# Stick-breaking attention: suffix sums as pairs of float32r matmuls, the mask added on TensorE, and the weights kept in softplus form

## The reference

```
z = jnp.einsum('bqhd,bkhd->bhqk', qb, kk).astype(jnp.float32) * scale
...
mask = (k_pos[None, :] < q_pos[:, None])[None, None]
log_beta = jax.nn.log_sigmoid(z)
log_one_minus = jnp.where(mask, jax.nn.log_sigmoid(-z), 0.0)
suffix = lax.cumsum(log_one_minus, axis=3, reverse=True) - log_one_minus
A = jnp.where(mask, jnp.exp(log_beta + suffix), 0.0)
outs.append(jnp.einsum('bhqk,bkhd->bqhd', A.astype(v.dtype), vv))
```

## Time and profile before

| What | us |
|---|---|
| median of 3 runs | 4930.05 (4927.13 to 4930.28) |
| the profiled execution, its own time | 4933.49 |
| its span in the profile | 4931.4 |
| PE busy in the span | 4438.4 (90%) |
| DVE busy in the span | 2837.3 (58%) |
| ACT busy in the span | 1843.0 (37%) |

### The profile page before, as it was taken

One profiled execution on the slowest core, in us unless ns is written; L12 is line 12 of the kernel. 1 busy time (PEld: TensorE's weight loads), 2 busy tenths in 40 slices (PEclk: granted clock), 3 DMA queues, 4 the chain that ended last, 5 costly groups with the idle time before them and its releaser, 6 DMA issues. The chain is left out here.

```text
span 4931.4 us, 59891 instructions
## 1 busy us (share of the span) xinstructions
PE 4438.4 (90%) x22171; PEld 3698.0 (75%) x22171; DVE 2837.3 (58%) x5051; ACT 1843.0 (37%) x2602; POOL 413.9 (8%) x308
## 2 busy tenths in 40 slices
PE   7988888878998466999999996999999999899998
PEld 5867775645874256999999995766878877677887
DVE  0777776683436897888888885334343333444332
ACT  1655644443321033333333333346232233643322
POOL 0000000000002601232222320000000000000000
PEclk9999999999999798999999998999999999999999
DMA  7111111102221036777777771211323322122232
GB/s 261 56 39 39 35 35 43 39 13 90 90 77 61 10 137 229 280 269 281 271 277 280 270 278 63 72 48 45 101 90 98 95 75 66 37 73 92 95 96 84
DMA packets 195952, 578.14 MB, mean 117 GB/s; under 512 B 17328, under 2 KB 66736, under 8 KB 194352
## 3 DMA queue, kind: packets, MB, share of 16 engines
q1 hardware_dynamic: 157888, 433.77, 25.9%
q0 software_dynamic: 36864, 134.23, 8.0%
q10 hardware_dynamic: 1008, 7.55, 0.4%
HBM read 548.22 MB, written 27.26 MB: 117 GB/s over the span
## 5 line engine op out<-in xcount | busy, mean ns | idle before, releaser
L402 DVE TENSOR_TENSOR tile_rest<-tile_raw,tile_up 128x1024 fp32r<-128x1024 f32 (+2 forms) x288 | 338.6, 1180 | 781.9 <-ACT tile_up L393 781.6
L410 PE MATMUL layer_psum<-hn_up,tile_up 128*128 128x512 f32 x1344 | 535.0, 398 | 21.2 <-DVE hn_rest L497 21.2
L411 PE MATMUL layer_psum<-hn_up,tile_rest 128*128 128x512 f32 x1344 | 527.3, 392 | 0.0
L412 PE MATMUL layer_psum<-hn_rest,tile_up 128*128 128x512 f32 x1344 | 527.0, 392 | 0.0
L393 ACT ACTIVATE tile_up<-tile_raw 128x1024 fp32r<-128x1024 f32 (+2 forms) x288 | 291.4, 1018 | 369.1 <-PE layer_psum L412 368.5
L2186 PE MATMUL ex_psum<-ex_t_up,ex_u_up 128*128 128x384 f32 x1024 | 344.5, 336 | 10.5 <-ACT ex_prod L2260 6.2
L2204 PE MATMUL ex_psum<-ex_prod_up,ex_v_up 128*128 128x384 f32 x1024 | 342.9, 335 | 3.9 <-DVE xT L2326 3.9
L2187 PE MATMUL ex_psum<-ex_t_up,ex_u_rest 128*128 128x384 f32 x1024 | 344.0, 336 | 0.0
L2188 PE MATMUL ex_psum<-ex_t_rest,ex_u_up 128*128 128x384 f32 x1024 | 343.9, 336 | 0.0
L2206 PE MATMUL ex_psum<-ex_prod_rest,ex_v_up 128*128 128x384 f32 x1024 | 342.6, 335 | 0.0
L2205 PE MATMUL ex_psum<-ex_prod_up,ex_v_rest 128*128 128x384 f32 x1024 | 342.6, 335 | 0.0
(11 more groups left out here) (440 smaller groups left out, 10140.1 us busy)
## 6 DMA issues: line engine op xcount, KB each, us to landing
ex_u<-in_peer_u SPq DMA_DIRECT2D x128, 512.0 KB, 6.8
tT<-in_peer_v SPq DMA_DIRECT2D x128, 512.0 KB, 7.4
tile_raw<-in_w_gu SPq DMA_DIRECT2D x88, 512.0 KB, 3.5
xT<-in_w_head SPq DMA_DIRECT2D x56, 512.0 KB, 3.5
mod_w<-in_w_ada SPq DMA_DIRECT2D x48, 512.0 KB, 4.8
mg_w_raw<-in_w_merge SPq DMA_DIRECT2D x48, 512.0 KB, 3.5
expert_table<-et_rows SPq DMA_DIRECT2D x6, 4096.0 KB, 13.3
ex_rows<-expert_table SPq DMA_DIRECT2D x64, 384.0 KB, 8.0
```

What stands on the lines that cost most here:

```text
L402: self.nc.vector.tensor_tensor(out=self.rest[:, n % self.SLOTS, 0:blocks, :], in0=self.raw[n % self.RAWS][:, 0:blocks, :], in1=self.up[:, ...
L410: self.nc.tensor.matmul(dst, w_up, up, start=first, stop=False)
L411: self.nc.tensor.matmul(dst, w_rest, up, start=False, stop=False)
L412: return self.nc.tensor.matmul(dst, w_up, rest, start=False, stop=last)
```

## The change

- **Softplus form.** With s = max(z,0) + ln(1 + exp(-|z|)), which is -log_sigmoid(-z), the weight is exp(z - sum of s over this key and all later ones). `later` now has 1 on its diagonal too, so the key's own term is inside the sum.
- **The mask on TensorE.** After each score matmul a 128x128 float32r matmul (`far` times `later`, with minus sign) adds -2^30 on the masked places of the diagonal block, so that both s and the weight become 0 there. The two mask products on DVE and the constant `before` go.
- **Sums in float32r.** ACT rounds s to `up` (a new 128x1280 copy), DVE subtracts to get `low` (a new 128x1280 operation), and PE multiplies both with the negated constants: 20 float32r matmuls instead of 10 float32 ones. Three negated or scaled constants (`minus_later`, `minus_ones`, `minus_far`) are made once by ACT at the start of the first layer's stick-breaking, and the first scores wait for them.
- **No slices.** The PSUM places of a head are contiguous now. Abs reads all 1280 columns straight from PSUM, DVE copies them to `z`, and `powers` is three operations by bank. `scored` is raised once per head, after its last matmul.
- **Buffers.** `z` lies in the tile of the tables, so the tables are loaded again for the second layer. `o` lies in `beta` of head 0, so Abs of head 0 waits for `sb_rest` of the pair before.
- **Order.** On ACT the logarithm of head 0, then that of head 1, then the rounding of head 0; the rounding of head 1 stands after head 0's final Exp.

The core of the diff:

```diff
-                nc.tensor.matmul(part(hh, c), k[rows, c * P:(c + 1) * P], q[rows, c * P:T],
-                                 start=True, stop=True).then_inc(scored[hh], 1)
+                nc.tensor.matmul(part(hh, c), k[rows, c * P:(c + 1) * P], q[rows, c * P:T], start=True, stop=False)
+                ins = nc.tensor.matmul(part(hh, c)[:, 0:P], mem.minus["far"][:], mem.minus["later"][:],
+                                       start=False, stop=True)
+            ins.then_inc(scored[hh], 1)
...
-            pe.wait_ge(rested[hh], START + 3 * i + 3)
+            pe.wait_ge(low_ready[hh], START + i + 1)
...
-                    ins = nc.tensor.matmul(dst[:, (c2 - c) * P:T - c * P],
-                                           mem.c("later") if c2 == c else mem.c("ones"),
-                                           rest[hh][:, AT[c2]:AT[c2] + n], start=c2 == c, stop=c2 == TB - 1)
+                    sign = mem.minus["later"][:] if c2 == c else mem.minus["ones"][:]
+                    for piece in (up[hh], low[hh]):
+                        ins = nc.tensor.matmul(dst[:, (c2 - c) * P:T - c * P], sign, piece[:, AT[c2]:AT[c2] + n],
+                                               start=c2 == c and piece is up[hh],
+                                               stop=c2 == TB - 1 and piece is low[hh])
...
+            if i > 0 and hh == 0:
+                act.wait_ge(sb_cut, START + i)
+            nc.scalar.activation(beta[hh][:], every(hh), ACT.Abs).then_inc(soft[hh], 1)
...
+        def halves(i, hh):
+
+            act.wait_ge(raised[hh], START + i + 1)
+            nc.scalar.activation(up[hh][:], beta[hh][:], ACT.Copy).then_inc(up_ready[hh], 1)
...
+            exponentials(i, 0)
             logs(i, 0)
+            exponentials(i, 1)
             logs(i, 1)
...
+            halves(i, 0)
+            between(i, 0)
+            tile(i, 0)
+            weights(i, 0)
+            halves(i, 1)
+            between(i, 1)
+            tile(i, 1)
+            weights(i, 1)
...
+            copies(i, 0)
+            raises(i, 0)
+            copies(i, 1)
+            halves(i, 0)
+            raises(i, 1)
+            powers(i, 0)
+            tile(i, 0)
+            halves(i, 1)
+            tile(i, 1)
+            powers(i, 1)
```

More of the change, by code:

```diff
@@ L42 @@
 CONSTS = [("ones", P), ("mean_d", P), ("mean_head", P), ("mean_ret", P), ("ident", P), ("swap", P),
-          ("later", P), ("before", P), ("iota", P), ("eps", 1), ("one", 1),
+          ("later", P), ("iota", P), ("eps", 1), ("one", 1),
           ("cos2", T), ("sin2", T)]
@@ L2624, in vector @@
                 w.cut_rest(dve, n)
-            dve.wait_ge(tables, START + 16)
+        dve.wait_ge(tables, START + 16)
         for n in range(4):
@@ L2831, in output, with between, tile @@
             act.wait_ge(o_filled[hh], START + i + 1)
-            if i > 0:
-                act.wait_ge(sb_cut, START + i)
             nc.scalar.activation(o[rows, :], B[4 * hh][rows, :], ACT.Copy).then_inc(o_out[hh], 1)
+        def between(i, hh):
+            if i + 1 < PAIRS:
+                evacuate(hh, i + 1)
+            else:
+                sigmoid(hh)
+        def tile(i, hh):
+            w.cut_up(act, (Q_AT[i + 1] if i + 1 < PAIRS else mx) + 4 + hh)
+        if layer == 0:
+            nc.scalar.activation(mem.minus["later"][:], mem.c("later"), ACT.Copy, scale=-1.0).then_inc(signs, 1)
+            nc.scalar.activation(mem.minus["ones"][:], mem.c("ones"), ACT.Copy, scale=-1.0).then_inc(signs, 1)
+            nc.scalar.activation(mem.minus["far"][:], mem.c("ident"), ACT.Copy, scale=-FAR).then_inc(signs, 1)
         for i in range(PAIRS):
-            following = i + 1 < PAIRS
+            exponentials(i, 0)
             logs(i, 0)
+            exponentials(i, 1)
             logs(i, 1)
[L2840 to L2847, removed]
+            halves(i, 0)
[6 more added lines that the diff above has]
+            weights(i, 1)
             if i < 2:
@@ L2856, in scalar @@
                 act.wait_ge(o_out[hh], START + i + 1)
-            nc.scalar.activation(mem.sb_up[:, i, :], o[:], ACT.Copy).then_inc(sb_up_ready, 1)
+            nc.scalar.activation(mem.sb_up[:, i, :], o, ACT.Copy).then_inc(sb_up_ready, 1)
         w.cut_up(act, mx + 6)
     def vector(dve):
[L2862 to L2867, removed]
@@ L2879, in powers @@
         def powers(i, hh):
-            for c, made in zip(ORDER, MADE):
-                dve.wait_ge(summed[hh], START + i * TB + made)
-                cols = slice(AT[c], AT[c] + T - c * P)
-                nc.vector.tensor_tensor(out=beta[hh][:, cols], in0=beta[hh][:, cols], in1=part(hh, c),
+            for bank in range(3):
+                dve.wait_ge(summed[hh], START + i * 3 + bank + 1)
+                cols = slice(bank * 512, min(bank * 512 + 512, ALL))
+                nc.vector.tensor_tensor(out=z[hh][:, cols], in0=z[hh][:, cols], in1=every(hh)[:, cols],
@@ L3172, in phase_layers @@
                     with ExitStack() as own:
-                        ret = stage_retention(nc, io, mem, ph, allocator(own), layer, norm)
+                        ret = stage_retention(nc, io, mem, ph, allocator(own), layer, norm, stick)
                     with ExitStack() as own:
```

108 lines of the change are left out of this document (53 added, 55 removed).

## The result

| | us |
|---|---|
| median of 4 runs, changed kernel | 4974.45 (4967.57 to 4978.46) |
| kernel before, on the same chip | 4928.59 (4924.69 to 4930.28) |
| ratio, 95% interval | 1.0091 (1.0079 to 1.0103) |
| span of the profiled execution | 4976.7 (before 4931.4) |
| PE, DVE, ACT busy in the span | 4486.9, 2831.4, 1839.5 |

The change costs 46 us. I had forecast 17, with 4968 us as the upper end; the sign was right and the size outside my range. The 45.3 us between the two spans lie in the two touched stretches: the first layer's ends 26.8 us later than before (1.7 of them had gathered ahead of the stage), and the second adds 18.3. Behind each of the two stretches stands a small difference of 2 us, and these cancel.

The account below looks back on a forecast made before the run. Each pair was bound by the ACT and DVE path to head 0's sums, then PE's work from there. 38.2 - 28.8 + 1.2 = +10.6, plus 6.3 for the clock, gave +16.9: 4947 us, range 4935 to 4968.

Parts of the forecast that it names:

- the sign: Whole kernel: the change makes it slower, chance 0.76; within 0.17, faster 0.07.
- four mask matmuls of 0.09 (priced below) 0.36: Head 0's scores on PE: four masks at 0.09 us each add 0.36 us to 1.97 us of scores.
- the mask matmuls of head 1 lie in the idle time ahead of head 0's sums: PE ahead of head 0's sums: head 1's masks fall in idle time, so no cost was added for them.
- my 16.79: Second pair: head 0's sums start 16.79 us after the first score, against 12.28 before, 4.51 later.
- Part one: Start of head 0's sums: later in every pair, mainly by head 1's logarithm in the path; +38.2 us in all.
- Part two: PE's own work: float32r sums of 2.59 us instead of 4.39, 16 times, -28.8 us; waits before outputs +1.2 us.
- The float32-rate rival: Sums and masks on PE: narrow float32r matmuls run at the float32 rate; +37.7 us, so 4968 us; chance 0.14.
- Part three: PE's clock at head 0's sums: longer idle time makes restarts run at half clock; +6.3 us.
- low in all eight: Head 0's sums: after 6.35 us idle, all eight pairs restart at half clock, losing mean 2.0 us each.
- the clock term: Restarts of head 0's sums at half clock: 16.0 us lost against 9.7 before, +6.3 us.

Follow-up runs that it names:

- no_mask: The changed kernel without the eight mask matmuls per pair, so masked places keep their values; 4956.46 us, ratio 1.0052.
- mask_grouped: The changed kernel with scores of three blocks, their three masks, then the last score and mask, four changes a head instead of eight; 4961.22 us, ratio 1.0063.
- mask64_full: The changed kernel with each mask made of two 64-row matmuls instead of one of 128 rows, the second with constants turned by 64 rows; 4960.15 us.
- full_in_order: mask64_full_early with head 1's rounding ahead of head 0's weights on ACT and its remainder ahead of head 0's additions on DVE; 4930.98 us.
- mask64_full_early: mask64_full with head 0's rounding right behind head 1's Abs, and head 0's remainder ahead of head 1's copy; 4932.35 us, ratio 1.0008.

## Why the prediction was wrong

**The step that failed: "four mask matmuls of 0.09 (priced below) 0.36".** I priced a mask by its columns, as one more float32r matmul in a row of its own kind. It stands between matmuls of 64 rows, and each change costs 0.17 us. Head 0's scores and masks took 3.96 us, not 2.33. I also wrote that "the mask matmuls of head 1 lie in the idle time ahead of head 0's sums". PE's idle time did cover them, but ACT's path did not: ACT needs head 1's masked scores before head 0's rounding, and waited 1.48 us for them. At full clock they would have been ready in time; what I put at nothing is the fall of the clock inside them. The 1.63 and the 1.48 are 3.1 of the 3.2 us between my 16.79 and the measured 20.00 from the first score.

**Part one, head 1's logarithm in the path: right.** Without the masks 16.80 us in the second pair where I had 16.43 for that case. So the sign was no luck: no_mask, without any mask, is still 26 us slower than the kernel before. The first pair took 18.98, since its scores ran at half clock behind the wait for the constants. I had counted only the 2.5 us of a later start: 2.2 us more.

**Part two: near.** A head's sums at full clock 2.8 us instead of 2.59; the 384-column spacings (0.17) and the 128-column ones (0.09) were as taken, the rest stands at the changes of block. Head 1's sums didn't wait, as forecast. The float32-rate rival is out.

**Part three, the clock: right for long waits, but these were met elsewhere.** My forecast "low in all eight" belongs to a wait of 6.35 us. no_mask has it (7.1 us, 4.50 in the first pair; eight of eight at 0.50 to 0.56, about 2.2 us each where I had 2.0). The Trainium skill's page "TensorE: Matmul & The Clock Gate" (HAM oscillation) says the same of waits between bursts, and these eight agree. The changed kernel waits 1.6 to 2.7 us, and the sums were low in six of eight (not behind the waits of 1.64 and 1.72 us):

```profile
3309.25:3313.63 4.38, 4.38 (x20) 0.61 0.02 4
3396.41:3399.30 2.89, 2.89 (x21) 1.00 0.00 0
4384.34:4388.80 4.46, 4.46 (x21) 0.62 0.02 4
sum 31.67, PE 31.66; mean PE 3.96
```

These are the windows over head 0's sums, three of the eight and the sum of all. 31.67 us, before 44.53.

**The sum again, from the two traces.** The forecast stands in brackets. From the first score to head 0's sums, over eight pairs: 166.5 us after, 98.5 before, +68.0 (35.7). First score later behind the constants: +2.5 (2.5). Head 0's sums 31.7 - 44.5 = -12.9; head 1's 8 x (2.79 - 4.43) = -13.1; together -26.0 (with the clock term: -28.8 + 6.3 = -22.5). The outputs' waits at the end of the third and fourth pairs: -0.9 (+1.2), since in the third pair the wait of 0.45 us went away and only in the last it grew, to 0.72. Sum +43.6, and 1.7 had gathered ahead of the stage: the 45.3. So the whole miss is in the first term: 32 us, of which the trace of no_mask, with 135.5 us there, puts 31.0 on the masks. Its timelines of ACT, beside those of the changed kernel, divide them: over the eight pairs head 0's logarithm starts 15.3 us later behind its masked scores, and ACT then waits 13.8 us for head 1's (1.26 to 1.85 in each pair). With float32 masks, where head 1's took 4.43 us at full clock, ACT did not wait for them in any of the seven pairs. So some 12 of the 31 us, the waits in the seven pairs behind the first, go through the fall of the clock. That no_mask is only 18 us faster is part three: without masks PE waits longer and all eight sums fall to half clock.

**What stays open.** Why the clock falls in head 1's masked scores, behind no idle record. In the changed kernel they took 6.35 to 6.94 us in all eight pairs (in the first the clock was low from the start); with float32 masks 4.43 and with one 64-row mask a block 2.21 or 2.22, at full clock, in the seven pairs behind the first. The alternation of 64 and 128 rows alone is not it. With fewer changes (mask_grouped) the clock fell in two of those seven pairs, and with two 64-row masks a block and no change at all it fell in one of them in mask64_full, one in full_in_order and two in mask64_full_early. The kernel with float32 masks has as many changes as the changed one, and there it did not fall behind the first pair. What decides it was not measured.

## What to carry to other kernels

A matmul added between others is not priced by its own columns: see whether it changes the number of rows or the shape of its neighbours, and if so give it their rows. Here a mask of two 64-row matmuls added 0.25 us at full clock, one of 128 rows 0.50. When two independent chains share an engine, put each step that releases TensorE ahead of the other chain's longer steps, and follow it for every iteration, the last too, where other work stands between. And a wait of TensorE costs its length and the slower restart: 7.1 us of waiting came with 2.2 us more.

## What was not expected of the hardware

- A change between matmuls of 64 and 128 rows: 0.17 us at the full clock, twice per mask.
- The granted clock is 0.50 to 0.55 in head 1's masked scores of all eight pairs, while the records show PE busy without a gap; in seven of them it had been higher in head 0's. The busy column doesn't show this; the granted clock does. The same happened now and then between 64-row matmuls alone (0.65 over 8.46 us in mask64_full).
- 416 matmuls whose results nobody reads made a kernel 16 us faster, since they kept TensorE at 2.4 GHz across a 7 us wait.
